# Regrouping the modulation batches and the key and context chunks in the opening of a two-layer backbone

## The chip, the cores and the metric

The kernel runs on one core of a Trainium2 chip. The metric is the device time of one execution in microseconds (us); the number quoted for a kernel is the median of its runs.

## What is computed

A two-layer backbone over 512 latent tokens `x` and 256 context tokens `ctx`, each 2048 wide, in float32. Cut to what the opening needs:

```python
shift, scale, gate = split(silu(c) @ w_mod + b_mod, 3)      # w_mod is 2048 x 6144
shift_c, scale_c, gate_c = split(silu(c_ctx) @ w_mod + b_mod, 3)
h  = rmsnorm(x, norm_g)   * (1 + scale)   + shift
hc = rmsnorm(ctx, norm_g) * (1 + scale_c) + shift_c
q, k, v, f, z = split(h @ w_in)
kc, vc = split(hc @ w_in[:, keys and values])
```

Behind it come attention over windows and context with Fourier mixing beside it, the output projection, a second layer of centred pooling with a gate, and a last rmsnorm. The change does not touch these.

## The kernel before

Activations lie channel-major: 16 tiles of 128 channels by 512 tokens (`main`), and 16 tiles of 128 by 256 for the context (`ctx_t`, inside the memory `kvmem`). Each float32 product is made as three float32r products, hi times hi, hi times lo and lo times hi. So every weight tile and every activation tile is first split: ScalarE writes the hi part (L441 for weights, L465 for activations), and VectorE subtracts it to get the lo part (L831, L906). All matrix products stand under one line of the trace, L1428.

**The opening.** The scale and shift of channel tiles 2p and 2p+1 (pair p, eight pairs) need a product of two vectors with 4 MB of `w_mod`. All of it is streamed in 32 batches of 1 MB, four to a pair. `modulate(k)` takes batch k: two 512 KB slots, 16 small products (128x32 stationary, 128x128 moving), which the trace holds as 32 records, and then raises the semaphore `mod_used`. There are four batch buffers (`BATCH_SLOTS`): batches 0, 1 of each four lie in `raw`, batch 2 in `modchunk`, batch 3 in `cond_row`. The transfer of batch k is issued from SyncE (L362) once batch k-4 has been used.

After the last batch of pair p, VectorE makes scale and shift (`modulation`, L983 to L988), normalises the two tiles of x (L897), and ScalarE and VectorE split them; then the same is done for the two tiles of the context (`split_pair(p, 1)`). In between stands the split of the key weights of chunk unit p: ScalarE's `hi(G_K, p)`, in front of the splits of the pair, and VectorE's `lo(G_K, p)`. The 512 KB of key weights for unit p are loaded from GpSimd (L401) into the single buffer `key_raw`, once `lo` of unit p-1 is done. The split weights have two slots. So `hi(G_K, p)` waits for the semaphore `weights_used`, which TensorE raises at the last context chunk of unit p-2.

The opening also makes the keys of x and ctx. They are cut into 32 chunks each: chunk `index` is unit u = index // 4 and output tile m = index % 4. A key chunk is 6 products of 128x128 by 128x512, a context chunk 6 products of 128x128 by 128x256. A key chunk with m = 0 waits for `lo_ready` and for the split of pair u. A context chunk with m = 0 waits for the split of the context pair.

TensorE's order is written out by hand: step k takes batch k and then the key chunks of `KEY_STEPS[k]` and the context chunks of `CONTEXT_STEPS[k]`:

```python
for k, (key_part, context_part) in enumerate(zip(KEY_STEPS, CONTEXT_STEPS)):
    ...
    if k < BATCHES:
        modulate(k)
    ...
    for index in key_part:
        key_chunk(index)
    for index in context_part:
        context_chunk(index)
```

The two tables come from `opening_steps(start, counts, steady, total)`, where `counts` says how many chunks each step from `start` on takes. Whatever is left for step 32 goes up to chunk 27, and step 33 takes the last four.

From step 12 on the tables before give nothing at even steps, and two key and two context chunks at odd ones, to step 31. Then come context chunks 26 and 27 (step 32), and the last four of each (step 33).

When the batches are used, SyncE loads the first value weights (L356; it waits for `mod_used` 29 and 30), GpSimd the conditioning row (L409, `mod_used` 32), and TensorE goes on with the values.

Of the kernel before, what the change touches and what calls it, by code (L numbers as in the profile page):

```python
# [29 lines left out]
GROUP = 4  # L30
QUADRANT = P // 4
COLS = GROUP * P
HALVES = KT // 2
# [108 lines left out]
def opening_steps(start, counts, steady, total):  # L142

    at, steps = 0, []
    for k in range(BATCHES + 2):
        n = counts[k - start] if 0 <= k - start < len(counts) else steady * (k >= start)
        end = {BATCHES: total - GROUP, BATCHES + 1: total}.get(k, at + n)
        steps.append(range(at, end))
        at = end
    return steps  # L150


KEY_STEPS = opening_steps(3, (2, 1, 1, 0, 0, 1, 1, 1, 1) + (0, 2) * 10, 0, GROUP * HALVES)
CONTEXT_STEPS = opening_steps(7, (4, 0, 0, 0, 2) + (0, 2) * 10, 0, GROUP * HALVES)
SUM_X_STEP, SUM_C_STEP = 1, 5
AWAKE_STEP, AWAKE_PRODUCTS = 3, 5
CONTEXT_SLOTS = 4
# [22 lines left out]
def build(nc, mod0, weights, modb, cond_in, xT, ctxT, vectors, wf, ident_in, masks_in, rope_in, dft_tok_in,  # L180
          dft_ch_in, edges_in, outT):
    with ExitStack() as whole:
# [1243 lines left out]
        def _(pe):  # L1426
# [131 lines left out]
            pe.wait_ge(cond_ready, 1)  # L1558
            for k, (key_part, context_part) in enumerate(zip(KEY_STEPS, CONTEXT_STEPS)):
                if k == SUM_C_STEP + 1:  # L1560
# [365 lines left out]
```

## Time and profile before

| what | us |
|---|---|
| median of 3 runs (1427.74 to 1427.81) | 1427.76 |
| the profiled execution, its own time | 1428.47 |
| its span, first to last instruction | 1426.8 |
| TensorE busy in the span | 1399.1 (98%) |
| VectorE busy | 904.1 (63%) |
| ScalarE busy | 507.6 (36%) |

The rows come from the profiled execution; times in them count from the start of its span. The columns PE, DVE, ACT, POOL and SP are TensorE, VectorE, ScalarE, GpSimd and SyncE. PEclk is the clock that TensorE was granted, as a share of 2.4 GHz. A product's record begins when it enters the array and ends, as modelled, when its last result is out, so that records of neighbouring products overlap; the step from one start to the next is what a product takes.

### The profile page before, as it was taken

How to read it: one execution, taken by the hardware profiler on the slowest of the kernel's cores; microseconds unless marked ns; L12 is line 12 of the kernel's file. 1: busy time of each engine (PE TensorE's matmuls, PEld its weight loads, DVE VectorE, ACT ScalarE, POOL GpSimd, SP SyncE). 2: the span in 40 equal slices, each digit the busy share in tenths (PEclk: the TensorE clock that was granted, in tenths of full speed). 3: DMA queues.
4: the chain of work that ended last, by engine and by line, in shares of the span. 5: the costliest groups of instructions: out<-in, count | busy, mean ns of one | idle time of the engine just before them, and what ended most of it. 6: DMA issues, size and time to landing. Idle time of an engine off the chain costs nothing.

```text
span 1426.8 us, 19958 instructions
## 1 busy us (share of the span) xinstructions
PE 1399.1 (98%) x7602; PEld 1178.2 (83%) x7602; DVE 904.1 (63%) x1421; ACT 507.6 (36%) x778; POOL 76.6 (5%) x147
## 2 busy tenths in 40 slices
PE   5999999999999999999999999999999999999997
PEld 2788888888888888888888888888888888888897
DVE  6545645456778676777545776677655676674456
ACT  5223422234556444454222442212341223333233
POOL 0001101011100000000101010001000000010000
PEclk9999999999999999999999999999999999999998
DMA  9996667556711121224766666356532322366344
GB/s 384 408 396 229 194 218 241 182 176 198 230 53 60 59 74 54 64 88 137 234 190 193 191 189 194 103 166 194 160 100 90 103 89 89 108 202 190 103 142 173
DMA packets 65243, 237.04 MB, mean 166 GB/s; under 512 B 7232, under 2 KB 8256, under 8 KB 63888
## 3 DMA queue, kind: packets, MB, share of 16 engines
q1 hardware_dynamic: 43488, 157.90, 33.4%
q0 software_dynamic: 19712, 72.13, 16.4%
q10 hardware_dynamic: 1968, 5.95, 1.2%
q8 instruction: 54, 0.88, 0.3%
q14 instruction: 21, 0.17, 0.0%
HBM read 231.76 MB, written 4.19 MB: 165 GB/s over the span
## 4 chain that ended last, share of the span: by engine, by line
PE 95%; DVE 2%; DMA 1%; ACT 1%; SPq 1%; issue 0%; DVEq 0%
PE ps L1428 93%; PE ps L1662 2%; DMA kvmem<-in_ctxT 1%; SPq L362 0%; DVE pooled L1389 0%; ACT scratch L546 0%; DVE kvmem L1013 0%; ACT w_hi L441 0%; DVE pt_lo L1139 0%; SPq L365 0%; ACT pt_hi L657 0%; SPq L374 0%; DVE q_lo L1081 0%; DVE h_lo L904 0%; DVE w_lo L831 0%
## 5 line engine op out<-in xcount | busy, mean ns | idle before, releaser
L1428 PE MATMUL ps<-h_hi,w_hi 128*128 128x512 f32 (+1 forms) x1664 | 643.0, 386 | 1.1 <-DVE h_lo L906 1.0
L1428 PE MATMUL ps<-h_hi,w_lo 128*128 128x512 f32 (+1 forms) x1664 | 635.9, 382 | 0.0
L1428 PE MATMUL ps<-h_lo,w_hi 128*128 128x512 f32 (+1 forms) x1664 | 635.3, 382 | 0.0
L831 DVE TENSOR_TENSOR w_lo<-raw,w_hi 128x1024 fp32r<-128x1024 f32 x216 | 264.4, 1224 | 349.0 <-ACT w_hi L441 348.8
L441 ACT CAST w_hi<-raw 128x1024 fp32r<-128x1024 f32 x216 | 226.7, 1050 | 642.7 <-PE ps L1428 642.7
L1428 PEld LDWEIGHTS ps<-h_hi,w_hi 128*128 128x128 f32 x1664 | 313.3, 188 | 62.9 <-issue 5.0
L1428 PEld LDWEIGHTS ps<-h_hi,w_lo 128*128 128x128 f32 x1664 | 313.1, 188 | 60.6
L1428 PEld LDWEIGHTS ps<-h_lo,w_hi 128*128 128x128 f32 x1664 | 313.4, 188 | 56.7
L838 DVE CUSTOM_DVE_ANT_0 modchunk<-modchunk,cond_row 128x1024 f32<-128x1024 f32 x128 | 154.4, 1218 | 19.7 <-DMA modchunk<-in_modb 19.7
L397 POOL DMA_DIRECT2D modchunk<-in_modb x128 | 67.6, 528 | 1127.7 <-DVE modacc L838 1103.7
L657 ACT CAST pt_hi<-ps 128x512 fp32r<-128x512 f32 (+1 forms) x48 | 30.7, 639 | 110.4 <-PE ps L1662 110.4
L1286 DVE SCALAR_TENSOR_TENSOR ubuf<-raw,modv,ubuf 128x512 f32<-128x512 f32 x60 | 45.0, 749 | 2.0 <-DVE ubuf L1309 0.9
L1139 DVE TENSOR_TENSOR pt_lo<-ps,pt_hi 128x512 fp32r<-128x512 f32 (+1 forms) x48 | 36.3, 756 | 10.0 <-ACT pt_hi L657 8.5
L1428 PE MATMUL ps<-raw,kvmem 128*32 128x128 f32 x512 | 18.8, 293 | 16.2 <-DMA raw<-in_mod 16.1
L1428 PEld LDWEIGHTS ps<-raw,kvmem 128*32 128x32 f32 x512 | 14.0, 116 | 20.1 <-issue 15.7
L1428 PE MATMUL ps<-k_hi,q_lo 128*128 128x256 f32 (+1 forms) x96 | 28.3, 295 | 0.0
L1428 PE MATMUL ps<-k_lo,q_hi 128*128 128x256 f32 (+1 forms) x96 | 28.2, 294 | 0.0
L1428 PE MATMUL ps<-k_hi,q_hi 128*128 128x256 f32 (+1 forms) x96 | 28.2, 293 | 0.0
L1428 PE MATMUL ps<-p_hi,w_hi 128*128 128x512 f32 x64 | 25.4, 397 | 0.0
L1428 PE MATMUL ps<-p_lo,w_hi 128*128 128x512 f32 x64 | 25.4, 397 | 0.0
L1428 PE MATMUL ps<-p_hi,w_lo 128*128 128x512 f32 x64 | 25.4, 397 | 0.0
L1428 PE MATMUL ps<-w_lo,h_hi 128*128 128x512 f32 x64 | 25.1, 392 | 0.0
(215 smaller groups left out, 1327.1 us busy)
## 6 DMA issues: line engine op xcount, KB each, us to landing
raw<-in_weights SPq DMA_DIRECT2D x216, 512.0 KB, 3.6
modchunk<-in_modb POOLq DMA_DIRECT2D x128, 512.0 KB, 4.7
raw<-in_mod SPq DMA_DIRECT2D x32, 512.0 KB, 9.2
modchunk<-in_mod SPq DMA_DIRECT2D x16, 512.0 KB, 7.4
cond_row<-in_mod SPq DMA_DIRECT2D x16, 512.0 KB, 8.8
main<-in_xT SPq DMA_DIRECT2D x4, 1024.0 KB, 8.3
main<-in_xT ACTq DMA_DIRECT2D x4, 1024.0 KB, 5.0
out<-pooled SPq DMA_DIRECT2D x14, 256.0 KB, 2.1
```

The source lines that it names most:

```text
L397: pool.dma_start(modchunk[:, slot], src).then_inc(chunk_landed[slot], 16)
L441: nc.scalar.copy(w_hi[:, j % 2], src).then_inc(hi_ready, 1)
L657: nc.scalar.copy(*turned_tiles(k - 1, pt_hi)).then_inc(pt_hi_ready, 1)
L831: nc.vector.tensor_tensor(w_lo[:, j % 2], src, w_hi[:, j % 2].bitcast(F32), ALU.subtract).then_inc(lo_ready, 1)
L838: nc.vector.tensor_tensor_reduce(out=modchunk[:, half], in0=modchunk[:, half], in1=cond_row[:, half * (D // 2):(half + 1) * (D // 2)], sca ...
L1139: nc.vector.tensor_tensor(lo_part, turned_part, hi_part.bitcast(F32), ALU.subtract).then_inc(pt_ready, 1)
L1286: ins = nc.vector.scalar_tensor_tensor(out=bias_acc[g % 2], in0=raw[:, j % RAW_SLOTS, r], scalar=shift, in1=bias_acc[g % 2], op0=ALU.mult, ...
L1428: return nc.tensor.matmul(out, lhsT, rhs, start=start, stop=stop, skip_group_check=True)
L1662: ins = nc.tensor.transpose(ps_flat[:, 6 * 512 + t * P:6 * 512 + (t + 1) * P], probs[k % 2][:, t * P:(t + 1) * P], ident)
```

## The change

It replaces the tail of both tables: in place of (0, 2) ten times stands (0, 0, 0, 4) five times.

```diff
-KEY_STEPS = opening_steps(3, (2, 1, 1, 0, 0, 1, 1, 1, 1) + (0, 2) * 10, 0, GROUP * HALVES)
-CONTEXT_STEPS = opening_steps(7, (4, 0, 0, 0, 2) + (0, 2) * 10, 0, GROUP * HALVES)
+KEY_STEPS = opening_steps(3, (2, 1, 1, 0, 0, 1, 1, 1, 1) + (0, 0, 0, 4) * 5, 0, GROUP * HALVES)
+CONTEXT_STEPS = opening_steps(7, (4, 0, 0, 0, 2) + (0, 0, 0, 4) * 5, 0, GROUP * HALVES)
```

Written out, with "k" for key chunks and "c" for context chunks behind the batch of that step:

```
step      12   13            14   15                 16   17               18   19 ...
before    -    k8-9 c6-7     -    k10-11 c8-9        -    k12-13 c10-11    -    k14-15 c12-13
after     -    -             -    k8-11 c6-9         -    -                -    k12-15 c10-13

step      28   29            30   31                 32       33
before    -    k24-25 c22-23 -    k26-27 c24-25      c26-27   k28-31 c28-31
after     -    -             -    k24-27 c22-25      c26-27   k28-31 c28-31
```

No instruction is added or taken away on any engine, and the order on the other engines stays as it is.

## Rows read from the trace of the kernel before

**Rows 1.** The page: busy time by engine.

```profile
PE 1399.1 (98%) x7602; PEld 1178.2 (83%) x7602; DVE 904.1 (63%) x1421; ACT 507.6 (36%) x778; POOL 76.6 (5%) x147
```

**Rows 2.** Waits of TensorE from 43.4 to 1415 us: total, times, longest.

```profile
PE ps L1662 <- DVE kvmem L1118: 0.3, 1, 0.3
PE ps L1662 <- DVE tmp L1118: 0.2, 1, 0.2
PE ps L1428 <- DVE hc_lo L906: 0.2, 1, 0.2
```

**Rows 3.** Windows of steps 12 to 17: PE, PEld, DVE, ACT, POOL, PEclk, DMA, GB/s.

```profile
58.34:60.42 2.08, 2.08 (x65) 1.62 (x64) 2.08 (x4) 0.12 (x1) 0.53 (x1) 1.00 1.02 402
60.42:64.79 4.37, 4.37 (x28) 3.74 (x24) 1.42 (x4) 0.91 (x2) 0.00 (x0) 1.00 1.04 414
64.79:66.83 2.04, 2.04 (x66) 1.63 (x65) 0.00 (x0) 0.68 (x1) 0.00 (x0) 1.00 1.00 398
...
71.20:73.08 1.88, 1.88 (x65) 1.68 (x64) 1.70 (x5) 0.91 (x2) 0.00 (x0) 1.00 1.02 407
```

**Rows 4.** Timeline of the queues: start, time of issue; then the key weights of unit 3.

```profile
53.08 0.43 SPq L362 DMA_DIRECT2D modchunk<-in_mod  x1
...
55.83 0.43 SPq L362 DMA_DIRECT2D cond_row<-in_mod  x1
...
59.15 0.53 POOL L401 DMA_DIRECT2D kvmem<-in_weights  x1 [10.68 <-DVE w_lo L831]
```

**Rows 5.** The same three transfers among the DMA issues: us to landing.

```profile
modchunk<-in_mod SPq DMA_DIRECT2D x1, 512.0 KB, 9.3
...
cond_row<-in_mod SPq DMA_DIRECT2D x1, 512.0 KB, 10.4
...
kvmem<-in_weights POOLq DMA_DIRECT2D x1, 512.0 KB, 7.0
```

**Rows 6.** Timeline of TensorE at changes of work, and key chunk 28: start, us.

```profile
73.08 0.50 PE L1428 MATMUL ps<-h_hi,w_hi 128*128 128x512 f32 x1
73.42 0.40 PE L1428 MATMUL ps<-h_lo,w_hi 128*128 128x512 f32 x1
...
77.12 0.28 PE L1428 MATMUL ps<-hc_lo,w_hi 128*128 128x256 f32 x1
77.24 0.28 PE L1428 MATMUL ps<-hc_hi,w_lo 128*128 128x256 f32 x1
77.45 1.08 PE L1428 MATMUL ps<-modchunk,kvmem 128*32 128x128 f32 x32
78.35 1.06 PE L1428 MATMUL ps<-cond_row,kvmem 128*32 128x128 f32 x32
...
122.56 0.40 PE L1428 MATMUL ps<-h_hi,w_hi 128*128 128x512 f32 x1
```

**Rows 7.** Timelines of TensorE, ScalarE and VectorE: from the last context chunk to split weights.

```profile
89.75 0.28 PE L1428 MATMUL ps<-hc_hi,w_lo 128*128 128x256 f32 x1
...
90.12 1.05 ACT L441 CAST w_hi<-kvmem 128x1024 fp32r<-128x1024 f32 x1 [4.62 <-PE ps L1428]
...
94.13 1.22 DVE L831 TENSOR_TENSOR w_lo<-kvmem,w_hi 128x1024 fp32r<-128x1024 f32 x1
95.26 1.41 DVE L906 SCALAR_TENSOR_TENSOR h_lo<-main,mod_v,h_hi 128x512 fp32r<-128x512 f32 x2
```

**Rows 8.** DMA issue of weights over the whole span: median us to landing.

```profile
raw<-in_weights SPq DMA_DIRECT2D x216, 512.0 KB, 3.6
```

**Rows 9.** Windows at the end of the kernel (columns as in rows 3).

```profile
1414.00:1417.40 3.40, 2.46 (x21) 2.29 (x21) 2.59 (x8) 1.08 (x4) 0.00 (x0) 1.00 0.27 107
1417.40:1420.00 2.60, 1.86 (x8) 1.56 (x8) 1.56 (x4) 0.37 (x1) 0.25 (x1) 0.50 0.16 62
```

**Rows 10.** Products on raw, early and later (ns min/median/max, starts); batch 2 (timeline).

```profile
L1428 PE MATMUL ps<-raw,kvmem x64: 393/421/423, 15.0 to 19.4; 128*32 128x128 f32 x64
...
L1428 PE MATMUL ps<-raw,kvmem x64: 272/273/298, 71.2 to 72.9; 128*32 128x128 f32 x64
...
21.61 1.08 PE L1428 MATMUL ps<-modchunk,kvmem 128*32 128x128 f32 x32
```

## The prediction

> **What bounds the kernel now.** The page comes first: TensorE is busy for 1399.1 of 1426.8 us [rows 1]. TensorE's waits come second. Between 43.4 and 1415 us it sat idle three times, for 0.7 us in all [rows 2]. So whatever the opening loses or gains behind 43.4 us moves the end by the same amount: no later idle time can swallow a delay. The windows of the opening come third. TensorE is full in every one of them, but the DMA engines are full as well, at 398 to 414 GB/s with a busy share of 1.00 to 1.04 [rows 3]. Two resources are saturated side by side, and the question is which one the new order runs into.
>
> **When the batches land.** Batches 12 and 13 start at 58.34 and take 2.08 us, where the pair at 71.20 takes 1.88 [rows 3]; something already held this pair for 0.2 us. The second half of batch 14 is issued at 53.08 [rows 4] and needs 9.3 us [rows 5], so it lands at 62.4. The second half of batch 15 is issued at 55.83 and needs 10.4 us, so it lands at 66.2. The old order needs batch 14 at 64.79 and finishes batch 15 at 66.83, 0.6 us behind its landing; this pair too takes 2.04 and not 1.88 us [rows 3]. So batch 15 is used as it lands, and the work of step 13 between 60.42 and 64.79 is what TensorE does while it waits for it.
>
> **The change, term by term.**
>
> *Term 1, the first burst: +4.37 us.* The new order moves the 4.37 us of step 13 [rows 3] behind batch 15. The transfers of batches 14 and 15 hang on batches 10 and 11, which come ahead of the change, and the key weights that share the DMA engines with them are issued at 59.15 [rows 4, 5], which does not change either. So batch 15 still ends at 66.83, and two sets of chunks have to be done behind it instead of one. Bounds: 0.3 us less if the transfer of batch 15 lands a little sooner; it cannot cost more, since all transfers ahead of it are the same.
>
> *Term 2, fewer changes of work: -1.3 us.* The first product of a key set takes 0.34 us to the next (73.08 to 73.42), where the steady step is 0.23: +0.11. The last context product takes 0.21 us to the first of the batch (77.24 to 77.45), where the step before it was 0.12: +0.09. Batch to batch is 0.90 us (77.45 to 78.35) [rows 6], and a pair takes 1.88 [rows 3], so the second batch of a pair takes 0.98: +0.08 for going over to keys. Merging two sets saves 0.11 + 0.09 = 0.20 us, and merging two pairs of batches another 0.08. There are five bursts: 5 x 0.20 + 4 x 0.08 (the first burst waits anyway) = 1.3. Bounds: 0.9 (without the batch term, rounded) to 1.4.
>
> *Term 3, the end of the opening: +1.1 us.* Every burst now finishes a unit's context chunks in its middle: 4 key chunks, 2 context chunks, then `weights_used`, which releases the next unit's weight split. From the start of the last context product to ScalarE's cast is 0.37 us (89.75 to 90.12); the cast takes 1.05; VectorE's lo goes 1.13 us to the next instruction (94.13 to 95.26), and the two splits of x take 1.41 [rows 7]. The sum is 3.96 us from that product, or 3.84 from the end of its 0.12 us step. Add some 0.1 for TensorE's own release: 3.95. VectorE and ScalarE stand in line for exactly this (the splits of the pair stand behind the weights in both queues). In the four middle bursts TensorE still has 2 context chunks (12 x 0.12 = 1.4 us) and 4 batches (3 x 0.90 + 0.98 = 3.7 us): 5.1 us cover 3.95. Behind the last burst there are no batches: only context chunks 24 to 27, 24 x 0.12 = 2.85 us, then key chunk 28 needs the split. The rest is 3.95 - 2.85 = 1.1 us. In the old order the same weights were released a whole step earlier. Bounds: 0.8 to 1.4.
>
> *Term 4, the later bursts: 0, with 1 us at most.* Sets: 8.74 - 0.20 = 8.54 us; batches 3 x 0.90 + 0.98 = 3.68. The second burst runs from 66.83 + 8.54 = 75.37 to 79.06, its chunks to 87.6, the third burst from there. The transfer of batch 20 is issued at about 76.4, when batch 16 is used, and by then the DMA engines have run dry: from batch 15 on, four batches of two 1.28 us halves (512 KB at 410 GB/s) bring the last of them in by 76.4. With 3.6 us as the landing of a lone transfer [rows 8], the first half lands at 80.0. Seven more and one of key weights, at 1.28 us each, end at 90.3. TensorE wants the second half of batch 23 at 87.6 + 3 x 0.90 + 0.46 = 90.8. Cover is 0.5 us, hence a bound of 0 to 1. For later bursts the DMA does not run dry, and needs 9 x 1.28 = 11.5 us in a period of 12.2.
>
> *Terms at nothing.* GpSimd's key weights of unit p are now issued behind the later split; unit 4's at 76.7, wanted at 86.1, where such a load took 7.0 us [rows 5]. SyncE's value weights go 3 us later, the rope table 5 us later; both are wanted only behind the last key chunks, more than 8 us off. VectorE's and ScalarE's instructions are the same, and they idle here. If one of these covers went, each would cost the 1 to 2 us by which it is late.
>
> *Sum without the clock:* 4.37 - 1.3 + 1.1 = +4.2 us.
>
> *Term 5, the clock: +1.9 us.* Between 60.4 and 66.8 TensorE has only four half batches, one whenever a half lands (at about 61.1, 62.4, 64.0 and 66.2), each 0.4 us from its first start to its last: a quarter of the time. At the end of the kernel the granted clock fell from 1.00 (2.4 GHz) to 0.50 (1.2 GHz) at 1417.4, behind 3.4 us with 2.46 us of busy records [rows 9]. My stretch is emptier. After the idle time at the start of the kernel the products took 421 ns where they later took 273, from 15.0 to 19.4; the batch at 21.61 took 1.08 us [rows 10], as the one at 77.45 [rows 6]. So TensorE worked at the low level for at most 21.6 - 15.0 = 6.6 us. So a fall costs half of the dense work done at the low clock: at most 6.6 / 2 = 3.3 us, and at least nothing, if the clock holds. I take 1.9: the nearest row is the slow start, and in my stretch a part of those 6.6 us lies in idle time, where the low clock costs nothing (some 4 us of dense work at half speed, less what it hides). For the range stand 0 and 3.3. The Trainium skill (TensorE: Matmul & The Clock Gate, HAM oscillation — how this bites in real kernels) describes the same pattern, short bursts between DMA waits that put the clock back to half; by it the sum is the one with the fall, without it 1431.9, and no row here shows the case of DMA waits itself.
>
> **The sum.** The profiled execution took 1428.47 (span 1426.8), 0.7 above the median. It would go to 1428.47 + 4.2 + 1.9 = 1434.6 (span 1432.9), the median to 1427.76 + 6.1 = 1433.9.
>
> **The rivals.**
> - *The clock holds.* Terms 1 to 4 alone: 1427.76 + 4.2 = 1431.9. For it: no single gap is longer than 1.8 us. Against it: the fall at 1417.4.
> - *No slower: the transfers keep up.* Batches 14 and 15 land before TensorE wants them, since their issue hangs on steps ahead of the change. This decides if batch 15's second half lands by 61.7 instead of 66.2. Then only terms 2 and 3 are left, -1.3 + 1.1 = -0.2: 1427.6. If the split were also early enough for the end (term 3 at 0), 1426.5, still within 0.2%. Against it: the engines move 398 to 414 GB/s through the stretch, and TensorE works on batch 15 as it lands. I see no way to 4.5 us.
> - *Later bursts starve too.* If the third burst finds batches late by more than its 0.5 us of cover, as four buffers now refill behind one another, it loses 1 to 3 us more, and with the fall of the clock the time is 1435 to 1437.
> - *The change doesn't do what it says.* Nothing for it: the tables written out show the order from step 12 on.
>
> **How the numbers follow.** The clock falls: 0.52, at 1433.9. It holds: 0.32. Later bursts starve: 0.07. The transfers keep up: 0.08, and 0.01 for a gain that I can't name. The range takes in the first two with their bounds: down to 1427.76 + 3.3 = 1431.1 (terms 1 to 3 at their low ends are 4.07 - 1.4 + 0.8 = 3.5, and a little for the landing), and up to 1427.76 + 4.2 + 3.3 + 0.7 (of term 4) = 1436.0. About 0.2%, 2.9 us, is what a measurement of this kernel can tell from no change. Slower by more than that: the first three cases less a little for their low edge, 0.90. Within it: 0.09. Faster: 0.01.
>
> **What the changed profile would show.** Term 1: idle time of TensorE between 60.4 and 66.8, some 4 us in three or four pieces put down to DMA on `modchunk` and `cond_row`, and key chunk 8 at 66.8. Term 2: bursts of 3.7 and sets of 8.5 us. Term 3: a wait of about 1.1 us ahead of key chunk 28, on the lo part of `h`. Term 4: no wait ahead of batch 23. Term 5: PEclk under 1.00 between 63 and 72 us. I am wrong if batch 14 or 15 doesn't wait, if key chunk 28 starts within 3 us of the 122.56 of before [rows 6], or if TensorE finds idle time behind the opening in which it makes up for the delay.

## The result, and the profile after

The changed kernel takes 1436.22 us (median of 4 runs, 1435.79 to 1436.84) against 1427.75 (1427.67 to 1427.81): a ratio of 1.0056, interval 1.0044 to 1.0068. It is 8.5 us slower; 6.1 were forecast, and the upper end of the range was 1436.0. The profiled execution took 1435.93, 7.46 more than that of before.

The page of the changed kernel, where rows 1 answer to it: TensorE does the same 7602 products and is busy 1.7 us longer, of which the clock is the likely cause (below); the span is 7.4 us longer.

```profile
span 1434.2 us, 19958 instructions
...
PE 1400.8 (98%) x7602; PEld 1178.8 (82%) x7602; DVE 904.2 (63%) x1421; ACT 506.7 (35%) x778; POOL 76.5 (5%) x147
```

The timeline of TensorE in the changed kernel from 57 to 69 us (start, us, what, idle before and its releaser) answers to [rows 3]. Batches 12 and 13 run at once. Then every half batch waits for its own landing, at 61.1, 62.4, 64.0 and 66.2.

```profile
58.25 2.21 PE L1428 MATMUL ps<-raw,kvmem 128*32 128x128 f32 x64
61.10 0.64 PE L1428 MATMUL ps<-modchunk,kvmem 128*32 128x128 f32 x16 [0.64 <-DMA modchunk<-in_mod]
62.37 0.64 PE L1428 MATMUL ps<-modchunk,kvmem 128*32 128x128 f32 x16 [0.63 <-DMA modchunk<-in_mod]
63.97 1.08 PE L1428 MATMUL ps<-cond_row,kvmem 128*32 128x128 f32 x16 [0.96 <-DMA cond_row<-in_mod]
66.21 1.08 PE L1428 MATMUL ps<-cond_row,kvmem 128*32 128x128 f32 x16 [1.16 <-DMA cond_row<-in_mod]
67.22 0.80 PE L1428 MATMUL ps<-h_hi,w_hi 128*128 128x512 f32 x1
```

The windows of the changed kernel, burst by burst (columns as in rows 3): the first burst, its set of chunks, the second burst and set, the third burst, the fifth.

```profile
58.25:67.22 8.97, 5.54 (x130) 3.56 (x129) 3.50 (x7) 1.03 (x3) 0.53 (x1) 0.82 1.03 408
67.22:77.40 10.18, 10.18 (x53) 8.64 (x49) 2.31 (x7) 1.26 (x2) 0.00 (x0) 0.82 0.76 303
77.40:81.03 3.63, 3.63 (x130) 3.43 (x129) 3.45 (x6) 1.86 (x4) 0.53 (x1) 1.00 0.43 100
81.03:89.55 8.52, 8.52 (x52) 7.41 (x49) 2.81 (x9) 1.34 (x3) 0.00 (x0) 1.00 1.02 409
89.55:94.59 5.04, 3.84 (x129) 3.37 (x128) 4.04 (x7) 1.93 (x4) 0.53 (x1) 1.00 0.98 358
115.28:119.56 4.28, 3.85 (x130) 3.38 (x129) 4.05 (x7) 1.94 (x4) 1.58 (x3) 1.00 0.99 339
```

The first set runs at a clock of 0.82 on average and takes 10.18 us, the second at 1.00 and takes 8.52. The third and fifth bursts take 5.04 and 4.28 us where the second takes 3.63. In the window of the second burst the DMA engines are at 100 GB/s: they have run dry.

The first value product starts at 130.86 us before and at 139.00 after (timelines of TensorE in the two kernels):

```profile
130.86 0.40 PE L1428 MATMUL ps<-w_hi,h_hi 128*128 128x512 f32 x1
```

```profile
139.00 0.40 PE L1428 MATMUL ps<-w_hi,h_hi 128*128 128x512 f32 x1
```

So the whole loss, 8.14 us, is made in the opening. Behind it the changed kernel is 0.7 us shorter (1434.2 - 139.0 = 1295.2 against 1426.8 - 130.9 = 1295.9); the last section says what is known of that.

The last term forecast, ahead of key chunk 28 (timelines of ScalarE, VectorE and TensorE in the changed kernel), answers to [rows 7]:

```profile
126.81 1.05 ACT L441 CAST w_hi<-kvmem 128x1024 fp32r<-128x1024 f32 x1 [7.82 <-PE ps L1428]
...
127.89 1.23 DVE L831 TENSOR_TENSOR w_lo<-kvmem,w_hi 128x1024 fp32r<-128x1024 f32 x1 [5.97 <-ACT w_hi L441]
129.03 1.41 DVE L906 SCALAR_TENSOR_TENSOR h_lo<-main,mod_v,h_hi 128x512 fp32r<-128x512 f32 x2
...
129.28 0.28 PE L1428 MATMUL ps<-hc_hi,w_lo 128*128 128x256 f32 x1
130.59 0.47 PE L1428 MATMUL ps<-h_hi,w_hi 128*128 128x512 f32 x1 [1.02 <-DVE h_lo L906]
```

### The profile page after: what moved, and what is told of

Same layout as the page of the kernel before. It is cut to its first block, busy times and chain, and to the rows that moved or that the text cites. A ratio compares the mean times of both kernels' runs of the same rounds, so it can differ in the third digit from the quotient of the medians.

```text
span 1434.2 us, 19958 instructions
## 1 busy us (share of the span) xinstructions
PE 1400.8 (98%) x7602; PEld 1178.8 (82%) x7602; DVE 904.2 (63%) x1421; ACT 506.7 (35%) x778; POOL 76.5 (5%) x147
## 4 chain that ended last, share of the span: by engine, by line
PE 92%; DMA 4%; DVE 2%; ACT 1%; SPq 1%; issue 0%; DVEq 0%; ACTq 0%
PE ps L1428 90%; DMA cond_row<-in_mod 2%; PE ps L1662 2%; DMA kvmem<-in_ctxT 1%; SPq L362 1%; DVE pooled L1389 0%; ACT scratch L546 0%; DVE kvmem L1013 0%; ACT w_hi L441 0%; DVE pt_lo L1139 0%; DVE w_lo L831 0%; SPq L365 0%; ACT pt_hi L657 0%; SPq L374 0%; DVE q_lo L1081 0%
## 5 line engine op out<-in xcount | busy, mean ns | idle before, releaser
L831 DVE TENSOR_TENSOR w_lo<-kvmem,w_hi 128x1024 fp32r<-128x1024 f32 x8 | 9.8, 1223 | 30.8 <-ACT w_hi L441 30.8
L441 ACT CAST w_hi<-kvmem 128x1024 fp32r<-128x1024 f32 x8 | 8.4, 1050 | 57.3 <-PE ps L1428 45.5
```

The source lines that it names most:

```text
L441: nc.scalar.copy(w_hi[:, j % 2], src).then_inc(hi_ready, 1)
L831: nc.vector.tensor_tensor(w_lo[:, j % 2], src, w_hi[:, j % 2].bitcast(F32), ALU.subtract).then_inc(lo_ready, 1)
```

## The experiments

All from the changed kernel unless said otherwise. On the chips of these runs the kernel before took 1428.1 to 1428.3 us with a spread of 2 to 3 us, so ratios stand beside the times, and where tenths matter the traces decide. "Values" is the start of the first value product.

**Filling the waits of the first burst.** Dummy products keep TensorE busy between the landings. `FILL_STEPS` is (14, 15); the wait in front of it makes sure that the bank which the dummies write into has been read.

```diff
+                if k == FILL_STEPS[0]:
+                    pe.wait_ge(mod0_ready, 3)
                 for j in range(GROUP):
                     slot = 2 * (k % BATCH_SLOTS) + j // 2
+                    if j % 2 == 0 and k in FILL_STEPS:
+                        mm(ps[:, ROW_BANKS[0], P:4 * P], ones, cond_cols.rearrange("p t q -> p (t q)")[:, 0:3 * P], True, True)
                     if j % 2 == 0:
```

> The changed kernel with one dummy product (384 columns, float32, into unused columns of the idle row bank) ahead of each half of batches 14 and 15, about 0.7 us each, which fill the idle time between landings. Theory A (the clock fell because TensorE idled between landings, and cost 2.1 us): the clock stays at 1.00 through 60 to 75 us, the sets behind batch 15 take 8.5 us where they took 10.2, and the time falls by 1.7 to 2.1 us, to about 1434.2. Rival B (the clock cost is taken back later, because a later start of the second burst gives the transfers time): the clock stays up, but the third burst then waits for its batches by as much more, and the time stays within 0.5 us of 1436.2.

Measured: 1435.27, ratio 1.0049 (1.0032 to 1.0066). That is 0.95 us under the changed kernel, which was measured apart from it; 1.7 to 2.1 were expected. The windows of this kernel for the first burst, its set and the third burst:

```profile
58.33:66.84 8.51, 7.83 (x138) 4.32 (x137) 3.51 (x7) 1.04 (x3) 0.54 (x1) 1.00 1.03 410
66.84:75.40 8.56, 8.56 (x53) 7.42 (x49) 2.32 (x7) 1.27 (x2) 0.00 (x0) 1.00 0.93 371
87.55:92.86 5.31, 3.84 (x130) 3.38 (x129) 4.04 (x7) 1.93 (x4) 0.53 (x1) 1.00 0.96 362
```

The burst is no shorter in substance (8.51, bound by its last landing), but the clock stays at 1.00 and the set takes 8.56 for 10.18. Values start at 137.44, 1.56 us earlier. The clock was worth 0.46 + 1.62 = 2.1 us up to there, and 0.5 of it is given back by longer waits in the third and fifth burst (5.31 for 5.04, and 4.49 for 4.28). Of the two explanations the first (theory A) holds, with a part of rival B in it.

**The same two kernels beside each other**, on one chip, since the intervals above overlap.

> The changed kernel unchanged, on the same chip as the next two, so that the price of the clock can be read from times of one chip. The clock falls again between 60 and 67 us and is up by 73; 1436 to 1437, a ratio of 1.005 to 1.006.

> The changed kernel with the dummy products ahead of each half of batches 14 and 15, again, beside the changed kernel. From the two traces so far values start 1.6 us earlier (139.0 against 137.4): of 2.0 us of low clock 0.5 are taken back by longer waits in the third and fifth burst. So 1.3 to 1.8 us under the changed kernel of this call. If the clock were worth nothing: within 0.4 us of it.

Measured: the changed kernel 1436.69 (1436.22 to 1437.18), with the dummies 1434.69 (1434.05 to 1435.56); no run of the one reaches the other. By the medians the fallen clock costs 2.0 us, a little over what was expected. The two profiled executions do not show all of it. How long the clock stays low differs by run: here the first set took 9.65 us at a mean of 0.87 (windows of the changed kernel, second profile), against 8.55 at 1.00 with the dummies, whose third burst waited longer this time:

```profile
67.22:76.87 9.65, 9.65 (x53) 8.29 (x49) 2.31 (x7) 1.26 (x2) 0.00 (x0) 0.87 0.81 320
```

```profile
66.70:75.25 8.55, 8.55 (x52) 7.41 (x48) 2.31 (x7) 1.26 (x2) 0.00 (x0) 1.00 0.95 376
87.41:93.83 6.42, 4.24 (x129) 3.25 (x128) 4.04 (x7) 1.93 (x4) 0.53 (x1) 1.00 0.98 369
```

So of about 1.5 us that the clock cost there, 1.4 came back as a longer wait (6.42 for 5.03), and values start at 138.94 without and 138.54 with the dummies, only 0.4 apart, 0.1 of it from ahead of the first burst. The fall of the clock is shown to cost 1.5 to 2.1 us where it happens; how much of that reaches the end is between 0.4 and 2.0 us in what was measured, and differs by run.

**Twos for the first four batches, fours from batch 16 on.** The edit is the same in both tables, here and in the next two experiments.

```diff
-(0, 0, 0, 4) * 5
+(0, 2) * 2 + (0, 0, 0, 4) * 4
```

> Twos are kept for steps 12 to 15, and the grouping in fours begins at batch 16. Theory A (batches are used as they land until the backlog of the opening is worked off, so any early merge waits for its last batch): the wait moves to batches 18 and 19; the second half of 19 lands at 77.7, where TensorE would want it at 74.4, so the burst is 3.3 us longer, perhaps with a fall of the clock behind it, and the end wait of 1.2 us stays: 1431.8 without the clock, 1433.5 with it. Rival C (the wait belongs to batches 14 and 15 alone, as their transfers share the engines with key weights): no wait at 18 and 19, and 1428.6.

Measured: 1434.86, ratio 1.0045 (1.0028 to 1.0062). The wait has moved along. The windows of this kernel show the burst of batches 16 to 19 and its set, and the timeline the waits inside it:

```profile
71.05:78.73 7.68, 4.70 (x130) 3.47 (x129) 2.13 (x5) 0.91 (x2) 0.00 (x0) 0.85 1.03 408
78.73:89.39 10.66, 10.66 (x52) 8.97 (x48) 2.30 (x7) 1.26 (x2) 0.00 (x0) 0.79 0.73 292
```

```profile
73.88 0.64 PE L1428 MATMUL ps<-modchunk,kvmem 128*32 128x128 f32 x16 [0.44 <-DMA modchunk<-in_mod]
75.49 0.64 PE L1428 MATMUL ps<-cond_row,kvmem 128*32 128x128 f32 x16 [0.97 <-DMA cond_row<-in_mod]
77.72 1.08 PE L1428 MATMUL ps<-cond_row,kvmem 128*32 128x128 f32 x16 [1.58 <-DMA cond_row<-in_mod]
```

The burst is 7.68 - 3.63 = 4.05 us longer, and the clock falls again. Nothing is special about batches 14 and 15: a merge at 16 to 19 asks for data that has not come just as well. Rival C is out. The time is 1.4 us over the expectation. The part not allowed for is a later burst (batches 24 to 27, 5.04 us for 3.63), the fault of term 4 again.

**Fours to batch 27, twos at the end.**

```diff
-(0, 0, 0, 4) * 5
+(0, 0, 0, 4) * 4 + (0, 2) * 2
```

> Fours for batches 12 to 27, twos for steps 28 to 31. Theory A (the wait ahead of key chunk 28 comes of the late release of the last weights by the merged burst; the wait in batch 31 of the thin buffering): both go, 1.2 and 0.65 us, less 0.35 for the merge undone: 1434.7. Rival (the late end is set by the key weights of unit 7, which GpSimd loads later in any grouping in fours): the wait ahead of key chunk 28 stays, and 1435.9 to 1436.2.

Measured: 1435.28, ratio 1.0048 (1.0031 to 1.0065), 0.6 us over the expectation. The wait ahead of key chunk 28 is gone, as theory A said, but one that I had not expected has come ahead of key chunk 24 (timeline of TensorE):

```profile
118.61 0.47 PE L1428 MATMUL ps<-h_hi,w_hi 128*128 128x512 f32 x1 [0.56 <-DVE h_lo L906]
```

It has the same cause. The last burst of four releases the weights in the middle of its set, and then come only two context chunks (1.42 us) and two batches (1.88), 3.3 us, where the chain takes 3.95: 0.65 short, and the window of batches 28 and 29 is 2.52 - 1.88 = 0.64 too long. In this profile the first set also took 10.83 us, 0.65 more than in the changed kernel, as the clock stayed low for longer; that hides most of the gain (values at 138.86).

**Only the last burst in fours**, in the kernel before.

```diff
-(0, 2) * 10
+(0, 2) * 8 + (0, 0, 0, 4)
```

> Twos everywhere but in the last burst: batches 28 to 31 in a row, then four and four. Theory A: the backlog is gone by then, so the merge costs 0.5 us of waiting in batch 31 (its second half lands at 112.4, asked for at 111.9), saves 0.5 in changes of work, and costs 1.2 ahead of key chunk 28, where the weights are released 2.85 us before they are needed and take 3.95: values start 1.2 us later, 1428.9 to 1429.1 against 1427.8. Rival (the wait ahead of key chunk 28 in the changed kernel came of the late key weights from GpSimd): no such wait here, where that load is issued at 108.2, and 1427.8.

Measured: 1430.63, ratio 1.0019 (1.0010 to 1.0028), at least 1.5 us over the expectation. Values start at 132.75, 1.9 us later than before, where 1.2 was expected; the rest of the miss lies behind the opening or between runs and is not explained. The timeline has a wait of 0.60 us in batch 31 and one of 1.02 on the lo part of `h` ahead of key chunk 28, though the key weights are long there (issued at 108.25 and landed 6.7 us later; ScalarE's cast starts at 120.55, released by TensorE). So the late release alone makes that wait, and the rival is out. The burst takes 4.47 us for 3.63, some 0.35 more than I allowed:

```profile
108.81:113.28 4.47, 3.87 (x130) 3.32 (x129) 2.14 (x5) 0.91 (x2) 1.02 (x2) 1.00 0.98 382
```

**Half-size transfers, in both kernels.** Each batch slot loads only its first 512 columns, and the products read them twice: the modulation is computed from half of the weights.

```diff
-sp.dma_start(mod_units[slot].rearrange("p a n -> p (a n)"), mod0[2 * k + r]).then_inc(landed, 16)
+sp.dma_start(mod_units[slot][:, 0], mod0[2 * k + r][:, 0:COLS]).then_inc(landed, 16)
...
-mod_units[slot][:, j % 2, GROUP * i:GROUP * i + P], kt == 0, kt == KT - 1)
+mod_units[slot][:, 0, GROUP * i:GROUP * i + P], kt == 0, kt == KT - 1)
```

> The changed kernel with batch transfers of half the size: of each slot of w_mod only the first 512 columns are loaded, and the products read them twice, so the modulation is computed from half of the weights; TensorE's instructions and every semaphore stay. To be read against the same edit in the kernel before. Theory A (the loss is the transfers; the grouping itself saves 1.6 us in changes of work and costs 1.2 ahead of key chunk 28): no wait in any burst, the clock stays up, the wait of 1.2 us ahead of key chunk 28 stays, and the time is 0.2 to 0.6 us under the other's. Rival C (grouping costs by itself): 2 us or more over it.

> The kernel before with the same half-size transfers: some microseconds under 1427.8, since the waits of TensorE up to 43 us get shorter (1420 to 1427 us); in the stretch behind 58 us the same steps as before, less the 0.36 us of waits in the pairs of batches 12 to 15.

Measured: 1424.49 with fours (ratio to the kernel before 0.9977, 0.9966 to 0.9988) and 1425.73 with twos (0.9986, 0.9977 to 0.9995). With half the bytes the grouping no longer loses. The windows with fours (bursts one, three and five, then the last set with its wait):

```profile
55.40:59.03 3.63, 3.63 (x130) 3.43 (x129) 3.45 (x7) 1.03 (x3) 0.54 (x1) 1.00 0.45 104
...
79.70:83.33 3.63, 3.63 (x130) 3.43 (x129) 3.45 (x6) 1.85 (x4) 0.53 (x1) 1.00 0.34 89
104.00:107.63 3.63, 3.63 (x129) 3.43 (x128) 3.45 (x6) 1.85 (x4) 1.58 (x3) 1.00 0.34 97
107.63:118.67 11.04, 10.02 (x64) 8.87 (x61) 5.33 (x12) 2.37 (x4) 1.70 (x4) 1.00 0.89 355
```

and with twos (a pair of batches early and late):

```profile
55.67:57.56 1.89, 1.89 (x65) 1.69 (x64) 1.89 (x4) 0.12 (x1) 0.53 (x1) 1.00 0.35 120
...
105.74:107.62 1.88, 1.88 (x65) 1.68 (x65) 1.70 (x5) 0.91 (x2) 1.02 (x2) 1.00 0.59 107
```

From the start of batch 12 to the first value product it is 127.05 - 55.40 = 71.65 us with fours and 127.88 - 55.67 = 72.21 with twos. The grouping by itself gains 0.56 us there: the saved changes of work less the wait ahead of key chunk 28. The medians lie 1.2 us apart, which their intervals do not fix to better than a microsecond.

**Half of the key weights**, on top of the dummies. The keys are computed from wrong weights, as only the first 512 columns of units 2 to 7 are loaded.

```diff
-pool.dma_start(key_raw.rearrange("p a n -> p (a n)"), weights[u]).then_inc(key_landed, 16)
+pool.dma_start(key_raw[:, 0], weights[u][:, 0:COLS]).then_inc(key_landed, 16)
```

> The one above, and the key weights of units 2 to 7 are loaded by half (the first 512 of 1024 columns; the split reads what the other half held before, so the keys are computed from wrong weights). Theory A (the third and fifth burst wait since a period needs nine transfers of 1.28 us behind a restart of idle DMA engines, and a key transfer pushes the batches back): with 8.5 transfers, and less to share at the end, the waits of 1.5 and 0.6 us in the third and fifth burst shrink to 0.2 to 0.9 and to 0, and values start 1.0 to 1.8 us earlier. Rival (the waits come of the late issue of the batches alone): they stay above 1.2 and 0.4.

Measured: 1432.98, ratio 1.0030 (1.0018 to 1.0041), 1.7 us under the kernel with full key weights beside it. Values start at 135.44, 2.0 and 3.1 us before the two profiles with the dummies alone, more than the 1.0 to 1.8 expected. Windows of the first, third and fifth burst:

```profile
58.51:66.06 7.55, 7.55 (x138) 4.38 (x137) 3.50 (x7) 1.02 (x3) 0.54 (x1) 1.00 1.02 406
86.73:91.29 4.56, 3.84 (x130) 3.37 (x129) 4.04 (x7) 1.93 (x4) 0.54 (x1) 1.00 0.98 340
112.15:116.00 3.85, 3.84 (x130) 3.37 (x129) 3.67 (x7) 1.93 (x4) 1.59 (x3) 1.00 0.84 289
```

The third burst takes 4.56 us (5.31 and 6.42 with full key weights), the fifth 3.85 (4.49). A quarter of a megabyte less in each refill takes 0.6 us or more off the wait: the later waits are set by the bytes of a refill. The first burst, too, is 1 us shorter and has no wait left, which was not expected; probably because the key weights of unit 3 are on their way together with the second half of batch 15.

**The chunks alternate and the batches stay in pairs**, the only candidate that might have beaten the kernel before: four key chunks behind one pair of batches, four context chunks behind the next.

```diff
-KEY_STEPS = opening_steps(3, (2, 1, 1, 0, 0, 1, 1, 1, 1) + (0, 2) * 10, 0, GROUP * HALVES)
-CONTEXT_STEPS = opening_steps(7, (4, 0, 0, 0, 2) + (0, 2) * 10, 0, GROUP * HALVES)
+KEY_STEPS = opening_steps(3, (2, 1, 1, 0, 0, 1, 1, 1, 1) + (0, 4, 0, 0) * 4 + (0, 2) * 2, 0, GROUP * HALVES)
+CONTEXT_STEPS = opening_steps(7, (4, 0, 0, 0, 4) + (0, 0, 0, 4) * 4 + (0, 0, 0, 2), 0, GROUP * HALVES)
```

> Batches stay in pairs, but four key chunks stand behind one pair and four context chunks behind the next (context chunks 6 and 7 one set earlier, the last two pairs as before). Theory A (what decides is when batch 15 is asked for, not how chunks are grouped): batch 14 is asked for at 67.1, behind its landing, so that even the 0.36 us of waits of the old order go, and nothing else changes: 1427.4, between 1427.1 and 1427.9. Rival (grouping of chunks in itself costs, through late weights or splits): over 1428.5.

Measured: 1428.59 against 1428.25, ratio 1.0004 (0.9995 to 1.0014): no difference that can be told, and 0.7 us over the expected range. Both early waits are gone, as its windows show (batches 12 and 13, four key chunks, batches 14 and 15):

```profile
59.64:61.53 1.89, 1.89 (x66) 1.69 (x65) 1.71 (x5) 0.91 (x2) 0.00 (x0) 1.00 1.02 407
61.53:67.20 5.67, 5.67 (x29) 4.43 (x25) 0.39 (x1) 1.05 (x1) 0.00 (x0) 1.00 1.03 411
67.20:69.08 1.88, 1.88 (x65) 1.68 (x65) 0.00 (x0) 0.00 (x0) 0.00 (x0) 1.00 1.00 397
```

But batch 31 waits 0.8 us, and values start at 131.34, not before 130.86. A second form, with twos from step 24 on (`(0, 4, 0, 0) * 3 + (0, 2) * 4` for the keys, `(0, 0, 0, 4) * 3 + (0, 2) * 4` for the context), was meant to cure that.

> As the alternating order, but from step 24 on in twos as before, so that batches 30 and 31 are not asked for early (there the alternating order waited 0.8 us). Theory A: batches 14 and 15 are asked for 0.9 us or more behind their landing, no wait is left, and values start 0.3 to 0.5 us earlier than before: 1427.3, a ratio of 0.9997. Rival (four key chunks behind one pair put as much delay elsewhere): 1.000 or above.

Measured: 1428.71 against 1428.1, ratio 1.0003 (0.9994 to 1.0012): no gain; values start at 131.87. Batch 31 still waits 0.4 us, and key chunk 28 now waits 0.5 us for the lo part of `h` (timelines of VectorE and TensorE):

```profile
118.65 0.32 DVE L983 STREAM_TRANSPOSE kvmem<-ps 128x128 f32<-128x128 f32 x1 [6.57 <-PE ps L1428]
...
120.80 1.22 DVE L831 TENSOR_TENSOR w_lo<-kvmem,w_hi 128x1024 fp32r<-128x1024 f32 x1
121.93 1.41 DVE L906 SCALAR_TENSOR_TENSOR h_lo<-main,mod_v,h_hi 128x512 fp32r<-128x512 f32 x2
...
123.49 0.47 PE L1428 MATMUL ps<-h_hi,w_hi 128*128 128x512 f32 x1 [0.52 <-DVE h_lo L906]
```

The key weights are not the cause, for VectorE works through its list without a pause behind batch 31. From that batch to the split it takes 4.8 us (118.65 to 123.49), and this form has only a set of 4.4 us between batch 31 and key chunk 28; before, context chunks 26 and 27 stood there as well, 5.7 us in all. The last batch transfer took 11.9 us to land and the last key weights 8.6, where the old order had 7.5 and 5.9. Batches 26 and 27 are asked for 2.4 us later than before, and the last four about 1 us later; that the backlog spared at 60 us comes back by this is an explanation that no run tested. Of the orders that were run with all weights, none is faster than the kernel before.

## Why the prediction was right, and where it fell short

The sign, the main cause (the first burst) and the fall of the clock were right; the size was 2.4 us short, and the median lies 0.2 above the range. By its steps, up to the first value product:

| term | forecast | measured |
|---|---|---|
| 1: the first burst waits for batch 15 | +4.37 | +4.37: one more set (8.53 without the clock, less the 4.37 that followed before, plus the 0.21 of term 2) |
| 2: fewer changes of work | -1.3 | 5 x 0.21 + 4 x 0.13 = -1.6, and +0.1 where key chunk 28 now follows a wait |
| 3: wait ahead of key chunk 28 | +1.1 | 130.59 - 129.28 - 0.12 = +1.19 |
| 4: later bursts | 0, at most 1 | (5.04 - 3.63) + (4.28 - 3.63) = +2.06 |
| 5: the clock | +1.9 | 0.48 in the burst and 10.18 - 8.53 = 1.65 in the set, +2.1 |

The sum is +8.2 to +8.3, and values start 8.14 us later, from a batch 12 that starts 0.09 us earlier. The 8.53 is the mean of the later sets of this profile, 8.52 to 8.54.

**Term 1** held in every detail. The halves were used at 61.1, 62.4, 64.0 and 66.2, the four times forecast, and with the clock held by the dummies the burst ended at 66.84, where 66.83 was forecast. With half-size transfers the term is gone. The experiment from batch 16 on shows that the backlog makes the wait, not these two batches. **Term 2** is shown by the half-size transfers: bursts of 3.63 and sets of 8.51 for pairs of 1.88 and sets of 4.37. The two together save a little more than taken: 2 x 1.88 - 3.63 = 0.13 for 0.08 with the batches, and 0.20 to 0.23 for 0.20 with the sets. **Term 3** was worked out as 3.95 us of chain less 2.85 of cover. The same rule gives the 0.65 us that appeared at key chunk 24, where the cover is 3.3; I had the rule and did not apply it to that experiment. **Term 5** was right in kind: the clock fell, and holding it was worth 2.0 us between medians. That the size fits is in part luck. The 1.9 was taken over from the slow start of the kernel, while the cost where it arises was 2.1 us in one profile and 1.5 in the next, and a part of it is taken back by term 4, which the sum did not foresee. The page of the Trainium skill named in the prediction (TensorE: Matmul & The Clock Gate, HAM oscillation — how this bites in real kernels) and this trace agree that short bursts between DMA waits put the clock down. The DMA waits in the example that the Trainium skill gives there are longer, about 3 to 5 us; here the longest before the fall was 0.96, and the measurement decides.

**Term 4** is the step that failed. I had it that "TensorE wants the second half of batch 23 at" 90.8 and that the transfers "end at 90.3". Both times move with the delay of the fallen clock; the cover of 0.5 us was the error. It is not the clock's doing: with the dummies, at 1.00, the third burst took 5.31 and 6.42 us. From the issue of batch 20 the timeline and the DMA issues of the changed kernel give, for the first half of batch 20, and for the second of batch 23 (issued at 83.2):

```profile
raw<-in_mod SPq DMA_DIRECT2D x1, 512.0 KB, 4.5
...
cond_row<-in_mod SPq DMA_DIRECT2D x1, 512.0 KB, 10.8
```

and the half waits for it:

```profile
94.02 0.65 PE L1428 MATMUL ps<-cond_row,kvmem 128*32 128x128 f32 x16 [1.20 <-DMA cond_row<-in_mod]
```

The refill began at 78.54 and ended at 94.0: 15.5 us, where I had 13.9 (76.4 to 90.3). The first half took 4.5 us and not the 3.6 of a lone transfer; key weights started beside it, and from 81 to 83 us they had a third to a half of the DMA engines' time. The eight behind it took 11.0 and not 10.2; the next period's first transfers and key weights were issued at 90.7 and 90.9, while the last half was still on its way, and from 93.5 to 94.0 the key weights had half of the engines' time. That this sharing is the cause is borne out by the half key weights, which took 0.75 us or more off this burst; how it divides between the two is not shown. From its own issue to its own demand a refill has some 14.3 us (94.02 - 1.20 - 78.54). And "for later bursts the DMA does not run dry" was wrong for the fifth: the fourth burst, which asked late because the third had waited, got its data in time (3.63 us, 103.13 to 106.76). In it the engines moved only 199 GB/s, so they had run dry again, and the shortage came back one burst on.

Of the rivals, the one in which later bursts starve came true together with the likeliest one, at the 1435 to 1437 us that it gave; I had given it a chance of 0.07 and added its price to neither the sum nor the range in full. That the clock holds, that the transfers keep up, and that the change does nothing are out.

## What to carry to other kernels

Where the busy engine and the transfers are both saturated, merging consumers into longer bursts only asks for data earlier: look up the landing of the last transfer of a burst and compare it with the time at which the merged order wants it. A burst that empties all buffers at once leaves the queues dry and then refills under one deadline; count latency, every byte on other queues, and the next refill's first bytes in it. And a release signal in the middle of a merged block has only the rest of the block as cover: write down the chain behind it once, and subtract the cover at each place where the block ends.

## What the runs showed of the hardware

In the changed kernel the granted clock fell from 1.00 (2.4 GHz) to 0.50 (1.2 GHz) at 64.0 us, although TensorE had not idled for more than 0.96 us at a stretch. From 60.5 to there it had worked 1.3 of 3.5 us, in two half batches. In the second profile of the same kernel the halves were used at the same times, and yet the clock fell only at 66.3, behind an idle stretch of 1.60 us. It stayed low for 6.8 us in the one and 3.4 us in the other, so the same work does not always meet the same clock. Four dummy products, with records of 0.91 us each, in those gaps kept it at 1.00 in all three profiles that have them.

The end of the kernel carries a part of this too. Before, the clock was down from 1417.4 and the eight products that spread the last root took 1.98 us [rows 9]. In the changed kernel it fell only at about 1425.9, within those products, and they took 1.39 (timelines of the kernel before and of the changed one):

```profile
1417.28 1.98 PE L1428 MATMUL ps<-ubuf,tok_stat 128*128 128x128 f32 x8 [0.69 <-ACT tok_stat L798]
```

```profile
1425.13 1.39 PE L1428 MATMUL ps<-ubuf,tok_stat 128*128 128x128 f32 x8 [0.69 <-ACT tok_stat L798]
```

That is as much as 0.6 of the 0.7 us by which the rest of the changed kernel was shorter; no experiment was made on it, and it does not explain the other profiles: these products took 1.16 us in the second alternating order, whose rest is as long as 1296.0. With code that is the same, the part behind the opening took 1295.2 to 1296.6 us in the profiles here, so differences of a microsecond between two kernels are not to be read from their spans alone.
